# Output product and expert choice of layer 0 rearranged: latent tiles first, choice among the context tiles, weights loaded a stage earlier

## The reference, cut to what matters

```python
out = jnp.einsum('bnf,fd->bnd', jnp.concatenate([attn, conv], axis=-1), p['w_o'])
...
x = x + g1 * mix
h = rmsnorm(x, p['norm2']) * (1 + sc2) + sh2
x = x + g2 * expert_choice_ffn(h, p['w_router'], p['w_gate'], p['w_up'], p['w_down'])
...
# inside expert_choice_ffn, t are the tokens of one group
aff = jax.nn.softmax(jnp.einsum('td,de->te', t, w_router).astype(jnp.float32), axis=-1)
g, idx = lax.top_k(aff.T, cap)
xe = t[idx]
```

## Time and profile before

| | |
|---|---|
| median of three runs (lowest, highest) | 2422.81 us (2421.34, 2426.01) |
| the profiled execution, its time | 2418.45 us |
| the profiled execution, its span | 2416.2 us |
| TensorE busy, share of the span | 2071.2 us, 86% |
| VectorE busy | 856.4 us, 35% |
| ScalarE busy | 459.9 us, 19% |
| DMA, mean rate | 166 GB/s |

### The profile page before, as it was taken

The page is one execution under the profiler, slowest core; times in us unless marked ns, Lnnn a source line. Parts: engine busy times, 40 slices in busy tenths (PEclk is TensorE's granted clock), DMA queues, the critical chain, the costliest instruction groups (busy, mean ns, idle before and its releaser), DMA issues. The chain is left out here.

```text
span 2416.2 us, 29877 instructions
## 1 busy us (share of the span) xinstructions
PE 2071.2 (86%) x12375; PEld 1487.6 (62%) x12375; DVE 856.4 (35%) x1667; ACT 459.9 (19%) x930; POOL 177.9 (7%) x150
## 2 busy tenths in 40 slices
PE   4999999839999987991899999936995369999996
PEld 1888788625666653440778787822433258778784
DVE  1243433455666651227222222226043632222221
ACT  1122221126566650110000000005101200000000
POOL 0000000000000000000012111123000010112111
PEclk7999999969999998995899999977897779999998
DMA  8111100157444214426568787633014756878781
GB/s 349 53 43 45 42 29 32 47 155 257 188 157 157 82 34 168 139 101 230 214 235 306 273 278 262 225 123 135 0 53 158 261 198 194 294 255 312 271 278 27
DMA packets 158447, 402.26 MB, mean 166 GB/s; under 512 B 12385, under 2 KB 30486, under 8 KB 152186
## 3 DMA queue, kind: packets, MB, share of 16 engines
q1 hardware_dynamic: 143018, 346.56, 39.7%
q0 software_dynamic: 15312, 54.03, 8.1%
HBM read 340.01 MB, written 60.84 MB: 166 GB/s over the span
## 5 line engine op out<-in xcount | busy, mean ns | idle before, releaser
L1510 PE MATMUL experts_gu<-experts_h_t,weights_w_gate 128*128 128x160 f32 x2048 | 302.2, 301 | 4.1 <-issue 4.1
L1510 PEld LDWEIGHTS experts_gu<-experts_h_t,weights_w_gate 128*128 128x128 f32 x2048 | 288.5, 192 | 19.1 <-issue 19.1
L1510 PE MATMUL experts_gu<-experts_h_t,weights_w_up 128*128 128x160 f32 x2048 | 299.1, 299 | 0.0
L1510 PEld LDWEIGHTS experts_gu<-experts_h_t,weights_w_up 128*128 128x128 f32 x2048 | 285.1, 190 | 0.0
L1534 PE MATMUL experts_dn<-weights_w_down,experts_hid 128*128 128x512 f32 x512 | 225.8, 594 | 0.0
L499 PE MATMUL proj_cv<-proj_h_t,w_in_w_in 128*128 128x128 f32 x1920 | 219.3, 275 | 0.0
L499 PEld LDWEIGHTS proj_cv<-proj_h_t,w_in_w_in 128*128 128x128 f32 x1920 | 218.1, 192 | 1.5 <-issue 0.5
L1575 DVE TENSOR_TENSOR experts_hid<-experts_act,experts_gu 128x160 f32<-128x160 f32 x128 | 41.1, 321 | 478.7 <-ACT experts_act L1564 478.7
L1564 ACT ACTIVATE experts_act<-experts_gu 128x160 f32<-128x160 f32 x128 | 38.8, 303 | 833.4 <-PE experts_gu L1510 833.4
L1534 PEld LDWEIGHTS experts_dn<-weights_w_down,experts_hid 128*128 128x128 f32 x512 | 94.8, 190 | 113.8 <-issue 113.8
L884 PE MATMUL attn_sc<-attn_keys_s,attn_q_s 96*128 96x512 f32 (+1 forms) x384 | 154.6, 539 | 3.8 <-DVE attn_pr_t L1017 2.7
(11 more groups left out here) (294 smaller groups left out, 2262.2 us busy)
## 6 DMA issues: line engine op xcount, KB each, us to landing
weights_w_gate<-w_gate_l SPq DMA_DIRECT2D x32, 2048.0 KB, 9.2
weights_w_up<-w_up_l SPq DMA_DIRECT2D x32, 2048.0 KB, 15.9
weights_w_down<-w_down_l SPq DMA_DIRECT2D x32, 2048.0 KB, 19.6
attn_w_mod<-w_mod_l SPq DMA_DIRECT2D x40, 1024.0 KB, 6.4
mod_w_mod<-w_mod_l SPq DMA_DIRECT2D x8, 1024.0 KB, 8.0
xh_sample<-weights_w_down SPq DMA_DIRECT2D x16, 512.0 KB, 2.8
w_in_w_in<-w_in_l SPq DMA_DIRECT2D x3, 2048.0 KB, 19.9
proj_x<-x POOLq DMA_DIRECT2D x10, 512.0 KB, 3.6
```

The lines of the kernel that those rows point to most:

```text
L1510: last = pe.matmul(gu[j % 2][:, m * SLOTS:(m + 1) * SLOTS], w[u][:, k, j * P:(j + 1) * P], h_t[u][:, k, :], start=(k == 0), stop=(k == KD ...
```

## The change

The two stages of layer 0 share one new buffer, `Room`, of 32 KB on each partition, which is allocated before the attention and lives until the layer's end, in a stage of its own. In the attention SP issues the load of the output weights into it when it comes to slot 64, after the modulation's tasks. In the expert stage the same buffer holds the gate rows, the fetched tokens and the rows to be written.

`route` is no longer used for layer 0; `output_and_choice` takes its place, with the ten tiles written out one by one, the eight latent tiles first, the two context tiles last. The router of a tile runs in four column groups: the eight parts of the channels are spread over four groups of 16 output partitions (32 apart), which add up on their own; a copy of four tiles with the bias, four transposes, and a sum over the four groups on VectorE follow for each batch of tiles (4, 4 and 2). The choice among the latent tokens begins after the eighth tile and is interleaved by hand with the work of the two context tiles. SP asks for expert 0's weights at the fourth tile, for gate and up of expert 1 at the sixth, and for its down matrix at the end. Layer 1 keeps `route`.

```diff
+                    if n == SLOTS_N - HEADS:
+                        room.load_output_weights(sp, t)
...
+class Choice:
...
+    R, Q = 32, 4
+    TILES, CONDITION = (4, 4, 2), (1, 1, 0)
...
+    def route(self, pe, m, xh_t):
+        b, pos = divmod(m, 4)
+        c = self.CONDITION[b]
+        if m == 0:
+            pe.wait_ge(self.bias_kept, 1)
+            pe.wait_ge(self.prepared, 3)
+        if pos == 0:
+            wait(pe, self.lg_kept, b)
+        for k in range(KD):
+            q = k % self.Q
+            last = pe.matmul(self.lg[self.R * q:self.R * q + NE, pos * P:(pos + 1) * P], self.w_rs[:, c, k, :], xh_t[:, k, :],
+                             start=(k < self.Q), stop=(k >= KD - self.Q), skip_group_check=True)
+        last.then_inc(self.lg_full, 1)
+
+    def turn_batch(self, pe, b):
+        pe.wait_ge(self.lg_kept, b + 1)
+        wait(pe, self.wide_kept, self.WIDE_TURN[b])
+        for j in range(self.TILES[b]):
+            last = pe.transpose(self.wide[:, j * P:(j + 1) * P], self.lg_sb[:, j * P:(j + 1) * P], self.per.ident[:])
+        last.then_inc(self.wide_full, 1)
...
+    def keep_batch(self, act, b):
+        c, n = self.CONDITION[b], self.TILES[b] * P
+        act.wait_ge(self.lg_full, sum(self.TILES[:b + 1]))
+        if b:
+            act.wait_ge(self.wide_full, self.WIDE_TURN[b - 1] + 1)
+        act.activation(self.lg_sb[:, 0:n], self.lg[:, 0:n], ACT.Identity, bias=self.bias[:, c:c + 1]).then_inc(self.lg_kept, 1)
...
+    def rounds(self, dve, ch, c, lo, hi):
+        best, at, left = self.best[c], self.at[c], self.left[c]
+        for r in range(lo, hi):
+            src = left if r else self.aff[c]
+            eight = slice(8 * r, 8 * r + 8)
+            ch.link(dve.max(best[:, eight], src[:]))
+            ch.add(dve.max_index(at[:, eight], best[:, eight], src[:]))
+            if r < best.shape[1] // 8 - 1:
+                ch.add(dve.match_replace(left[:], best[:, eight], src[:], -1.0))
+            ch.settle()
...
+    def load_output_weights(self, sp, t):
+        sp.dma_start(self.room[:], t["w_o_l0"].rearrange("(k p) f -> p k f", p=P)).then_inc(self.w_o_in, 16)
...
+    ORDER = list(range(PT, NT)) + list(range(PT))
...
+                mixed(0)
+                choice.load(sp)
+                residual(0)
+                for c in (1, 0):
+                    sp.dma_start(gate[:, c, :], t["mod_rows_l0"][c, 2 * D:3 * D].partition_broadcast(P)).then_inc(gate_in, 16)
+                mixed(1)
+                residual(1)
+                for m in range(2, NT):
+                    mixed(m)
+                    residual(m)
+                    store(m - 2)
+                    if m == 3:
+                        weights.load(sp, 0)
+                    if m == 5:
+                        weights.load_gate_up(sp, 1)
+                store(NT - 2)
+                store(NT - 1)
+                sp.wait_ge(ms_ready, NT)
+                weights.load_down(sp, 1)
...
+                choice.make_bias(pe)
+                pe.wait_ge(room.w_o_in, 16)
+                product(0, 0, 0, KD)
+                product(0, 1, 0, KD)
+                for m in range(1, NT):
+                    product(m, 0, 0, KD)
+                    if m < NT - 1:
+                        turn(m - 1)
+                        product(m, 1, 0, 4)
+                        router(m - 1)
+                        product(m, 1, 4, 6)
+                        if m in (4, 8):
+                            choice.turn_batch(pe, m // 4 - 1)
+                        product(m, 1, 6, KD)
+                    else:
+                        choice.turn_affinities(pe, 1)
+                        product(m, 1, 0, 4)
+                        turn(m - 1)
+                        product(m, 1, 4, KD)
+                        router(m - 1)
+                turn(NT - 1)
+                router(NT - 1)
+                choice.turn_batch(pe, 2)
+                choice.turn_affinities(pe, 0)
+                choice.turn_lists(pe)
...
+                for m in range(ST):
+                    square(m)
+                    turned(m)
+                    if m in (3, 7):
+                        choice.keep_batch(act, m // 4)
+                choice.exponentials(act, 1)
+                square(ST)
+                turned(ST)
+                square(ST + 1)
+                turned(ST + 1)
+                choice.keep_batch(act, 2)
+                choice.exponentials(act, 0)
...
+                for m in range(ST):
+                    residual(m)
+                    normalise(m)
+                    turned(m)
+                    if m in (3, 7):
+                        choice.add_parts(dve, m // 4)
+                choice.shift(dve, ch, 1)
+                residual(ST)
+                choice.divide(dve, ch, 1)
+                normalise(ST)
+                choice.keep_affinities(dve, ch, 1)
+                choice.rounds(dve, ch, 1, 0, 3)
+                turned(ST)
+                choice.rounds(dve, ch, 1, 3, 6)
+                residual(ST + 1)
+                choice.rounds(dve, ch, 1, 6, 8)
+                normalise(ST + 1)
+                choice.rounds(dve, ch, 1, 8, 10)
+                turned(ST + 1)
+                choice.rounds(dve, ch, 1, 10, 12)
+                choice.add_parts(dve, 2)
+                choice.shift(dve, ch, 0)
+                choice.rounds(dve, ch, 1, 12, 13)
+                choice.divide(dve, ch, 0)
+                choice.rounds(dve, ch, 1, 13, 14)
+                choice.keep_affinities(dve, ch, 0)
+                choice.rounds(dve, ch, 1, 14, 16)
+                choice.rounds(dve, ch, 0, 0, CAP_P // 8)
+                choice.write_lists(dve, ch)
+                choice.write_tables(dve, ch)
...
-        attention(nc, t, per)
-        channel_mixer(nc, layer_0, per, 0)
+        with Stage(nc, "layer0") as u:
+            room = Room(u)
+            attention(nc, t, per, room)
+            with Stage(nc, "weights0") as v:
+                weights = Weights(v, t, 0)
+                output_and_choice(nc, layer_0, per, room, weights)
+                experts(nc, layer_0, per, 0, weights, room)
```

More of the change, by code:

```diff
@@ L749, in _, with attention @@
                     keys_kept(n, TP * NT + 2 * c + 1)
-def attention(nc, t, per):
+def attention(nc, t, per, room):
     K = (ST + CT) * P
@@ L1368, in load, with experts @@
         self.load_down(eng, e)
-def experts(nc, t, per, layer, weights):
+def experts(nc, t, per, layer, weights, room=None):
     BATCH = 4
@@ L1377, in experts @@
     with Stage(nc, f"experts{layer}") as s:
-        gate = s.sb("gate", [P, 2, D])
-        xs = [s.sb(f"xs{u}", [P, D]) for u in range(2)]
-        xp = s.sb("xp", [P, D])
+        gate = room.room[:, 0:2, :] if room else s.sb("gate", [P, 2, D])
+        xs = [room.room[:, 6 + u, :] if room else s.sb(f"xs{u}", [P, D]) for u in range(2)]
+        xp = room.room[:, 5, :] if room else s.sb("xp", [P, D])
         h_t = [s.sb(f"h_t{u}", [P, KD, SLOTS]) for u in range(2)]
@@ L1384, in experts @@
         hid = [s.sb(f"hid{b}", [P, KF, SLOTS]) for b in range(BATCH)]
-        ys = [s.sb(f"ys{u}", [P, D]) for u in range(2)]
-        yp = s.sb("yp", [P, D])
+        ys = [room.room[:, 2 + u, :] if room else s.sb(f"ys{u}", [P, D]) for u in range(2)]
+        yp = room.room[:, 4, :] if room else s.sb("yp", [P, D])
         tp = [s.ps(f"tp{b}") for b in range(2)]
```

242 lines of the change are left out of this document (added).

## The result

| | before | changed |
|---|---|---|
| median of four runs each (lowest, highest), us | 2424.41 (2421.34, 2431.03) | 2384.7 (2382.5, 2391.94) |
| ratio with 95% interval | | 0.9838 [0.9807, 0.9869] |
| the profiled execution, its span, us | 2416.2 | 2390.0 |
| stage's first load to the choice's last table (starts), us | 240.88 | 203.40 |
| from there to the first gate matmul, us | 18.06 | 17.99 |

Faster by 1.6%, and 0.9 us from the forecast of 2385.6. Part of that closeness is the base: the prediction counted from a median of 2422.81, which a fourth run of the kernel before moves to 2424.41, so the fall is 39.7 us where 37.2 was forecast.

A forecast was written before the change was run, and what follows sets the result against it. TensorE waits at the start and paces the product loop; VectorE alone bounds the choice. Start 13.3 plus loop and overlap 24.6 less 0.7 for a stage gives 37.2 us off the 2422.81 median: 2385.6 us, range 2377 to 2399.

The forecast's parts named there:

- Start: Product stage's start: with output weights loaded during attention, first output product at 905 instead of 918.3, 13.3 us earlier.
- The bounds of 903.5 to 908: First output product's start: 903.5 if only the tile counts, 908 if later gate broadcasts slow the landing.
- Router: Each tile's router in the product loop: four column groups abreast take 0.6 us instead of 1.85, saving 1.25.
- First product to E: Product loop, from first output product to the end of the ninth (first context tile): 140.6 us.
- E to the choice's end: From the ninth product's end to the complete choice: VectorE's program sets the end, 57.7 us.
- Expert loads hidden with 3 us to spare: Product loop: fifth activation tile lands behind expert loads 27.5 us after the second product, needed at 30.8.
- The price without cover, one for one: Product loop: expert loads that are not hidden cost one for one what they are late.
- One more stage: Layer 0's end: closing one more stage costs 0.7 us.
- Late tiles: Rival, product loop: activation tiles late behind expert weights; 10 us late loses 7, about 2393 us; chance 0.12.
- Serial groups: Rival, router: column groups do not run abreast, eight routers at 1.85 us, total about 2396 us; chance 0.10.
- A late start: Rival, stage start: router load or gate broadcasts hold the first tile; with 5 us left, 2394 us; chance 0.08.
- The clock: Rival, product loop: clock falls to the lower level, 15.4 us more per tile, four tiles near 2447; chance 0.04.

The follow-up runs named there:

- the second profile: The changed kernel run again unaltered: median 2385.75 us, ratio 0.9834 to the kernel before.
- e6: Changed kernel with the router's 16 bias products moved behind the first output product: median 2382.34 us, ratio 0.9827 to the kernel before.
- e9: Changed kernel with later bias products, less VectorE work, gathers free of bulk loads in both layers, and first latent tile loaded during attention: 2365.58 us.
- e2: Changed kernel with all eight router products of a tile in one column group, one after another: median 2398.0 us, ratio 0.9885 to the kernel before.
- e3: Changed kernel with all sixteen latent rounds after the whole work of the last two tiles: median 2400.84 us, ratio 0.9913 to the kernel before.
- e7: Changed kernel with context normalising and half the turned copy on ScalarE, softmax division and affinity turns earlier: median 2379.55 us, ratio 0.9808 to the kernel before.
- e5: Changed kernel with gate and up of expert 1 also asked for at the fourth tile: median 2395.66 us, ratio 0.9878 to the kernel before.
- e4: Changed kernel with expert 0's weights and expert 1's gate and up loaded after the last store: median 2381.03 us, ratio 0.9832 to the kernel before.
- e10: Changed kernel with output weights loaded at the product stage's start, router in one group, all latent rounds last: median 2421.23 us, ratio 0.9985 to the kernel before.
- e1: Changed kernel with output weights loaded first in the product stage, not in the attention: median 2395.37 us, ratio 0.9881 to the kernel before.

## Why the prediction was right, step by step

- *Start: 13.3 us foreseen, 11.8 measured* (12.5 in the second profile). This term was mis-sized. The tile was as foreseen (4.2 us after the first load; e6 has 3.97), but the router weights were charged the 2.4 us they took as the stage's first load, and took 4.6 as its third (906.03 to 910.66). The bounds of 903.5 to 908 held it: 6.4 us after the first load is 906.5 on that scale. Its place among the loads matters: as the third it took 3.2 to 5.6 us in the nine profiles that start alike, and 2.5 in e9, where it is the first again. Which of its neighbours slows it (the two halves of the tile ahead, the old stream and the gate rows behind), and why it varies so much in one place, was not settled.
- *Router: 0.6 us foreseen, 0.56 measured.* e2 gives its worth directly, 9.6 to 10.9 us over eight routers. Above the lower bound of 0.46 there is 0.10 left. The Trainium skill (TensorEngine Tiling (Array Packing), Key Properties) says that a change of mode drains the engine; if four groups take a quarter of the time of one, this trace leaves, at two changes a router, 0.05 us for each (an estimate).
- *First product to E: 140.6 foreseen, 140.7 measured* (139.4 in the second profile). The tile of 15.4 us is 15.37.
- *E to the choice's end: 57.7 foreseen, 56.5 measured* (1052.3 to 1108.76). The rounds began at E + 8.2, the figure of the sum. e3 and e7 confirm from both sides that VectorE's program sets this part: 13.2 us back when the rounds wait, 5.7 off when they begin sooner and work leaves VectorE.
- *Expert loads hidden with 3 us to spare.* e5 measured 3.0. The price without cover, one for one, was too low: 8.56 us of waiting cost 11.3, since the product behind it ran at a lower clock. e4 adds what the prediction left open: the move gains nothing.
- *One more stage: 0.7 us foreseen.* From the experts' last scatter to the next stage's first load it is 12.16 us against 11.94: 0.2, and 0.1 to 0.7 over all the kernels here.
- *The rivals.* Late tiles: no wait in the loop, and e5 shows what they would have looked like. (The 14.8 us by which the prediction has a tile late at the start are TensorE's whole idle time; the tile itself took 11.7 us to land, some 8 more than the usual 3.6.) Serial groups: refuted by 0.56 against 1.85. A late start: right in kind, through the router weights, but 0.8 to 1.5 us and not 8. The clock: 1.00 in the loop window.

Where the rest came from: e10 keeps 3.6 us. Its start accounts for 2.1 of them (16.13 against 18.23); the other 1.5, which should be the latent tiles' softmax and affinities done before the last tile, were not tried alone.

The three errors (start, choice, extra stage) were +1.5, -1.2 and -0.5 us in the first profile and cancelled in the sum. In the second the start missed by 0.8 and the loop came out 1.2 shorter, and the stretch fell by 39.6 us, as the medians did. The agreement to 0.9 us is closer than the terms deserve: that the errors cancel, and that the base moved by 1.6, is luck.

## What to carry to other kernels

When one engine limits a loop and another the work behind it, order the tiles so that an independent part of that work is ready early, and price the overlap from the first moment its data exist to the end of the second engine's program: that sum was good to 1.2 us in 57. Do not price a wait of TensorE by its length alone: the product behind it can run at a lower clock. Judge a change by the stage it touches, from one fixed instruction to another, because unchanged stages moved by up to 5 us between the profiles here. A bulk load that nothing waits for can still be in the way: look at which small transfers start in the same microseconds, and move the bulk.

## What the runs showed of the hardware that was not expected

- A gather takes more than twice as long when bulk loads run beside it: 9.42 us from its issue to the first transposes with two gate rows and two 2 MB matrices issued around it, 4.30 without them (9.23 and 4.17 in layer 1). The gathers are issued by GpSimd and the loads by SP, so separate issuers did not keep them apart. Which of the loads does it was not separated.
- The 64 KB router load took 2.4 us to land as the stage's first load (2.5 in e9), 3.2 to 5.6 as the third, and with the output weights ahead of it 13.5 (e1, 902.30 to 915.83). The size of a load said less than where it stood among the others.
- A single wait of 8.56 us in a loop that otherwise ran at clock 1.00 brought TensorE back at the lower level (1.2 GHz) for part of the next half product: 9.73 us instead of 7.03 (e5).
- Stages whose work is the same shifted: the product stage's first load came anywhere from 900.2 to 905.7 us in the kernels with the early weights and from 900.1 to 902.3 in the three without (before, e1, e10); two with the early weights, e3 and e4, are at 900.2, and in the first profile of the changed kernel the 5.1 us are there before the weights are asked for, so these don't explain it. The part from the Fourier mixer on ran from 802.6 to 807.0 us in the kernels that leave layer 1 as it was.
